# Output projection of a decoder layer with tokens on the partitions, and the first FFN tiles in token halves

## The reference, cut to what matters

```python
o  = m @ w_out                       # m: the merged mixers, (512, 1024); w_out: (1024, 1024)
x1 = x + o * rsqrt(mean(o * o, -1) + eps) * norm_post_mix
h2 = x1 * rsqrt(mean(x1 * x1, -1) + eps) * norm_pre_ffn
f  = (silu(h2 @ w_gate) * (h2 @ w_up)) @ w_down      # hidden width 2816
y  = x1 + f * rsqrt(mean(f * f, -1) + eps) * norm_post_ffn
```

## Time and profile before

| what | value |
|---|---|
| timed executions, median of 3 | 1194.46 us |
| the profiled execution's own time | 1198.94 us |
| its span in the trace | 1197.0 us |
| PE busy (matmul) | 1104.0 us, 92% |
| DVE, ACT, POOL busy | 575.0, 385.5, 504.9 us |
| share of PE in the chain that ended last | 61% |

### The profile page before, as it was taken

One profiled execution on the slowest core, in us unless ns is written; L12 is line 12 of the kernel. 1 busy time (PEld: TensorE's weight loads), 2 busy tenths in 40 slices (PEclk: granted clock), 3 DMA queues, 4 the chain that ended last, 5 costly groups with the idle time before them and its releaser, 6 DMA issues.

```text
span 1197.0 us, 19098 instructions
## 1 busy us (share of the span) xinstructions
PE 1104.0 (92%) x7610; PEld 851.6 (71%) x7610; DVE 575.0 (48%) x919; ACT 385.5 (32%) x679; POOL 504.9 (42%) x431
## 2 busy tenths in 40 slices
PE   5999898989996799999999899869999999999996
PEld 3775677777775566666767677747788788888885
DVE  4886745363564343445443676565344344331113
ACT  4122221212100433444443443244433433432222
POOL 1443322122233645665686445353444444434442
PEclk9998999999998999999999999979999999999998
DMA  7333112101143544122112436212233233222331
GB/s 216 92 88 71 51 31 51 23 19 29 55 124 106 167 127 125 53 54 62 28 36 62 149 115 202 71 53 67 85 94 101 83 97 97 81 67 89 96 91 75
DMA packets 172045, 101.30 MB, mean 85 GB/s; under 512 B 20997, under 2 KB 162575, under 8 KB 171976
## 3 DMA queue, kind: packets, MB, share of 16 engines
q1 hardware_dynamic: 168336, 95.44, 27.8%
q10 hardware_dynamic: 3608, 4.88, 1.7%
q0 software_dynamic: 32, 0.00, 0.0%
HBM read 92.67 MB, written 7.63 MB: 84 GB/s over the span
## 4 chain that ended last, share of the span: by engine, by line
PE 61%; issue 13%; DVE 11%; POOL 10%; ACT 2%; DMA 1%; POOLq 0%; DVEq 0%; ACTq 0%; SPq 0%
PE ps L1436 15%; PE ps L1438 13%; PE ps L1437 13%; POOL WLO L531 7%; PE ps L1569 5%; PE ps L1482 3%; PE ps L1721 2%; PE ps L1768 2%; DVE XF L1174 1%; DVE MT L1322 1%; POOL EB L592 1%; PE ps L1560 1%; DVE OT L1356 1%; POOL WLO L566 1%; DMA PRAW<-in_par 1%
## 5 line engine op out<-in xcount | busy, mean ns | idle before, releaser
L531 POOL TENSOR_TENSOR WLO<-WRAW,WHI 128x1024 fp32r<-128x1024 f32 (+3 forms) x156 | 331.2, 2123 | 390.2 <-ACT WHI L868 214.9
L1436 PE MATMUL ps<-HHI,WHI 128*128 128x512 f32 x792 | 331.5, 419 | 32.8 <-DVE HLO L1366 10.7
L1438 PE MATMUL ps<-HHI,WLO 128*128 128x512 f32 x792 | 311.8, 394 | 0.0
L1437 PE MATMUL ps<-HLO,WHI 128*128 128x512 f32 x792 | 311.7, 394 | 0.0
L1436 PEld LDWEIGHTS ps<-HHI,WHI 128*128 128x128 f32 x792 | 150.3, 190 | 99.3 <-issue 41.3
L1438 PEld LDWEIGHTS ps<-HHI,WLO 128*128 128x128 f32 x792 | 150.3, 190 | 33.0
L1437 PEld LDWEIGHTS ps<-HLO,WHI 128*128 128x128 f32 x792 | 150.6, 190 | 28.3 <-issue 2.3
L535 POOL CAST WHI<-WRAW 128x256 fp32r<-128x256 f32 (+1 forms) x83 | 48.9, 590 | 210.6 <-PE ps L1438 210.6
L868 ACT ACTIVATE WHI<-WRAW 128x1024 fp32r<-128x1024 f32 (+2 forms) x74 | 69.7, 941 | 137.2 <-PE ps L1438 137.1
L640 ACT ACTIVATE WHI<-WRAW 128x1024 fp32r<-128x1024 f32 (+1 forms) x57 | 50.0, 877 | 177.2 <-PE ps L1438 164.5
L1380 DVE TENSOR_TENSOR FT<-FT 128x512 f32<-128x512 f32 x22 | 38.5, 1750 | 110.3 <-ACT FT L874 110.3
(11 more groups left out here) (285 smaller groups left out, 1689.7 us busy)
## 6 DMA issues: line engine op xcount, KB each, us to landing
WRAW<-in_w_in SPq DMA_DIRECT2D x47, 512.0 KB, 4.1
WRAW<-in_w_gate SPq DMA_DIRECT2D x22, 512.0 KB, 3.8
WRAW<-in_w_up SPq DMA_DIRECT2D x22, 512.0 KB, 3.9
WRAW<-in_w_down SPq DMA_DIRECT2D x16, 384.0 KB, 3.4
spilled<-SQ SPq DMA_DIRECT2D x21, 256.0 KB, 2.3
WRAW<-in_w_down SPq DMA_DIRECT2D x16, 320.0 KB, 3.1
...
```

The source lines that it names most:

```text
L531: return pool.tensor_tensor(WLO[:, n % NSPL, 0:chunks, :], WRAW[:, n % NRAW, 0:chunks, :], WHI[:, n % NSPL, 0:chunks, :].bitcast(F32), ALU ...
L1436: pe.matmul(dst, WHI[:, s, k, :], hi, start=start, stop=False)
L1437: pe.matmul(dst, WHI[:, s, k, :], lo, start=False, stop=False)
L1438: return pe.matmul(dst, WLO[:, s, k, :], hi, start=False, stop=stop)
```

## The change

- The output product is turned round. The merged activations (MHI, MLO, a block of 128 tokens) become the stationary operand and 512 columns of `w_out` the moving one, so that a result bank holds 128 tokens on partitions by 512 channels (`out_product`, `out_bank`). A job is now two input chunks by 512 output columns. Jobs OUT0 to OUT0+3 make the left half of the channels for all four token blocks t at once, in four banks; jobs OUT0+4 to OUT0+7 make the right half, one token block after the other, in four further banks.
- Four more weight slots (XWHI, XWLO; `HOME`, `FREE`) hold jobs OUT0+2 to OUT0+5 and later FF0 and FF0+1, so that the weights of four jobs lie ready at once.
- The norm of a token block is a number per partition: ACT squares each bank with a sum along the free axis (`out_stats`), roots and reciprocals are of one column. `x_out(t)` on DVE scales from PSUM by that number and by the gain, read in by a DMA to all partitions (GPM). POOL adds XTOK in token layout; the result X1TOK is kept for the end of the kernel. The 32 transposes of x, the copies to OT and X1 and the sums in SSUM are gone, and so are the 32 transposes and 8 copies before the down stage.
- PE transposes X1TOK (`x1_transposes`), for token blocks 0 and 1 in the middle of the last block's output product, for blocks 2 and 3 after two half tiles of the FFN.
- HHI and HLO are made straight from PSUM in blocks of 256 tokens (`h2_high`, `h2_low`), and tiles FF0 and FF0+1 run as two halves of 256 tokens each.
- The second norm's factors (XRINV, one column per token block) are written on the diagonals of a matrix (DIAG, in SSUM) and spread over all partitions by one matmul with ones.
- The loads of x and of the gain are issued after the load of job OUT0+7, not after that of OUT0+3.

```diff
+HOME = {OUT0 + 2: NSPL, OUT0 + 3: NSPL + 1, OUT0 + 4: NSPL + 2, OUT0 + 5: NSPL + 3, FF0: NSPL, FF0 + 1: NSPL + 1}
+FREE = {OUT0 + 2: OUT0, OUT0 + 3: OUT0, OUT0 + 4: OUT0, OUT0 + 5: OUT0, OUT0 + 6: OUT0 + 1, OUT0 + 7: OUT0 + 2,
+        FF0: OUT0 + 3, FF0 + 1: OUT0 + 4, FF0 + 2: FF0, FF0 + 3: FF0}
...
-    OT = at("OT", 40, [P, KC, T])
-    X1 = at("X1", 116, [P, KC, T])
+    XWHI = at("XWHI", 40, [P, 4, 8, P], F32R)
+    XWLO = at("XWLO", 56, [P, 4, 8, P], F32R)
+    GPM = at("GPM", 16, [P, D])
+    OX = at("OX", 100, [P, 2, D])
+    X1TOK = at("X1TOK", 116, [P, 4, D])
...
-    X1TOK = Region(Z - 16 * KB).take("X1TOK", [P, 4, D])
...
+    def out_bank(t, dh):
+        return psum[(2, 3, 4, 5, 0, 1, 6, 7)[4 * dh + t]]
+    def x1_block(h, k):
+        return psum[(2, 3, 0, 1, 2, 3, 4, 6)[4 * h + k // 2]][:, 256 * (k % 2):256 * (k % 2) + 256]
...
-            return [(every, full, chunked(w_out, P * i))]
+            return [(every, full, chunked(w_out, T * (i // 4), T)[:, 2 * (i % 4):2 * (i % 4) + 2, :])]
...
-                if n == OUT0 + 3:
-                    sp.wait_ge(dense_done, OUT0)
-                    sp.dma_start(XTOK[:, :, :], x.rearrange("(t p) d -> p t d", p=P)).then_inc(xtok_in, 16)
+            sp.wait_ge(dense_done, OUT0)
+            sp.dma_start(XTOK[:, :, :], x.rearrange("(t p) d -> p t d", p=P)).then_inc(xtok_in, 16)
+            sp.dma_start(GPM[:, :], bass.AP(par1.tensor, par1.offset + P * PAR["g_post_mix"], [[0, P], [1, D]])).then_inc(gpm_in, 16)
...
                 if u == 2:
-                    for k in range(KC):
-                        pool.wait_ge(o_scaled, k + 1)
-                        pool.tensor_tensor(X1[:, k, :], X1[:, k, :], OT[:, k, :], ALU.add).then_inc(x1_ok, 1)
+                    pool.wait_ge(xtok_in, 32)
+                    for n in range(8):
+                        t, cols = n // 2, slice(T * (n % 2), T * (n % 2) + T)
+                        pool.wait_ge(ox_ok, n + 1)
+                        pool.tensor_tensor(X1TOK[:, t, cols], OX[:, t % 2, cols], XTOK[:, t, cols], ALU.add).then_inc(x1_ok, 1)
...
-                    act.wait_ge(dense_done, n - NSPL + 1)
+                    act.wait_ge(dense_done, slot_free(n))
...
-            for d in range(KC):
-                if n < FF0:
-                    hi_part(n)
-                    n += 1
-                act.wait_ge(dense_evac, group_of(OUT0 + d) + 1)
-                if d >= 2:
-                    act.wait_ge(out_sum, d - 1)
-                act.activation(SQ[:, d % 2, :], OT[:, d, :], ACT.Square).then_inc(out_sq, 1)
...
-            act.wait_ge(norm_ss, 2)
-            act.activation(SQ[:, 0, :], R[4][:, :], ACT.Sqrt, scale=1.0 / D, bias=EPSC[:, 0:1]).then_inc(norm_std, 1)
-            first_hi(1)
-            act.wait_ge(norm_rinv, 1)
-            for k in range(KC):
-                act.wait_ge(x1_ok, k + 1)
-                act.activation(HHI[:, k, :], X1[:, k, :], ACT.Identity, scale=par("g_pre_ffn", k)).then_inc(h2hi_ok, 1)
-                if k >= 2:
-                    act.wait_ge(x1_ss, k - 1)
-                act.activation(SQ[:, k % 2, :], X1[:, k, :], ACT.Square).then_inc(x1_sq, 1)
-            act.wait_ge(norm_ss, 3)
-            act.activation(SQ[:, 0, :], R[4][:, :], ACT.Sqrt, scale=1.0 / D, bias=EPSC[:, 0:1]).then_inc(norm_std, 1)
...
+            assert n == OUT0 + 2
+            for n in range(OUT0 + 2, FF0):
+                hi_part(n)
+            act.wait_ge(dense_done, OUT0 + 4)
+            for t in range(4):
+                if t >= 2:
+                    act.wait_ge(o_sq, t - 1)
+                act.activation(SQ[:, t % 2, :], out_bank(t, 0)[:, :], ACT.Square, accum_out=OSS[:, t:t + 1]).then_inc(o_sq, 1)
+            hi_part(FF0)
+            hi_part(FF0 + 1)
+            def out_stats(t):
+                if t < 3:
+                    act.wait_ge(out_t, t + 1)
+                else:
+                    act.wait_ge(dense_done, FF0)
+                act.wait_ge(o_sq, 3 + t)
+                act.activation(SQ[:, t % 2, :], out_bank(t, 1)[:, :], ACT.Square, accum_out=OSS[:, 4 + t:5 + t]).then_inc(o_sq, 1)
+                act.wait_ge(o_sq, 5 + t)
+                act.wait_ge(o_bias, 1)
+                act.activation(OSTD[:, t:t + 1], OSS[:, 4 + t:5 + t], ACT.Sqrt, scale=1.0 / D,
+                               bias=OBIAS[:, t:t + 1]).then_inc(o_std, 1)
+            def x1_stats(t):
+                act.wait_ge(x1_ok, 2 * t + 2)
+                act.activation(XTOK[:, t, :], X1TOK[:, t, :], ACT.Square,
+                               accum_out=XSS[:, t:t + 1]).then_inc(x1_sq, 1)
+            def h2_high(h):
+                act.wait_ge(x1T, 2 * h + 2)
+                for k in range(KC):
+                    act.activation(HHI[:, k, 256 * h:256 * h + 256], x1_block(h, k), ACT.Identity,
+                                   scale=par("g_pre_ffn", k)).then_inc(h2hi_ok, 1)
+            out_stats(0)
+            out_stats(1)
+            x1_stats(0)
+            out_stats(2)
+            x1_stats(1)
+            h2_high(0)
+            out_stats(3)
+            x1_stats(2)
+            h2_high(1)
+            x1_stats(3)
+            act.wait_ge(x1_sq, 4)
+            act.activation(XRINV, XSS, ACT.Sqrt, scale=1.0 / D, bias=EPSC[:, 0:1]).then_inc(x1_std, 1)
+            hi_part(FF0 + 2)
+            hi_part(FF0 + 3)
...
+            ffn_act(0, 0)
+            hi_loop(FF0 + 4, 0, 8)
+            hi_loop(FF0 + 5, 0, 8)
+            ffn_act(1, 0)
...
-            act.wait_ge(dense_done, DN0)
-            for n in range(0, 8, 2):
-                act.wait_ge(x1T, KC + n + 1)
-                act.activation(X1TOK[:, n // 2, 0:512], R[2 + n % 4][:, :], ACT.Copy).then_inc(tok_act, 1)
...
-            for d in range(KC):
-                if d == 5:
-                    for k in range(KC):
-                        dve.wait_ge(x1T, k + 1)
-                        dve.tensor_copy(X1[:, k, :], R[k % 4][:, :]).then_inc(x1T_ok, 1)
-                dve.wait_ge(dense_done, n + 1)
-                dve.tensor_copy(OT[:, d, :], DB[group_of(n) % 2][:, :]).then_inc(dense_evac, 1)
-                dve.wait_ge(dense_evac, group_of(n) + 1)
-                n += 1
-                if d == KC - 1:
-                    continue
-                dve.wait_ge(out_sq, d + 1)
-                if d == 0:
-                    dve.tensor_copy(SSUM[:, :], SQ[:, 0, :]).then_inc(out_sum, 1)
-                else:
-                    dve.wait_ge(out_sum, d)
-                    dve.tensor_tensor(SSUM[:, :], SSUM[:, :], SQ[:, d % 2, :], ALU.add).then_inc(out_sum, 1)
-            assert n == FF0
-            dve.wait_ge(norm_std, 2)
-            dve.reciprocal(RINV[:, :], SQ[:, 0, :]).then_inc(norm_rinv, 1)
+            dve.wait_ge(o_sq, 4)
+            dve.tensor_scalar(OBIAS, OSS[:, 0:4], 1.0 / D, EPS, ALU.mult, ALU.add).then_inc(o_bias, 1)
+            dve.wait_ge(gpm_in, 16)
+            def x_out(t):
+                dve.wait_ge(o_std, t + 1)
+                link(dve.reciprocal(ORINV[:, t:t + 1], OSTD[:, t:t + 1]))
+                for dh in range(2):
+                    if t >= 2:
+                        dve.wait_ge(x1_ok, 2 * (t - 2) + dh + 1)
+                    cols = slice(T * dh, T * dh + T)
+                    dve.scalar_tensor_tensor(out=OX[:, t % 2, cols], in0=out_bank(t, dh)[:, :], scalar=ORINV[:, t:t + 1],
+                                             in1=GPM[:, cols], op0=ALU.mult, op1=ALU.mult).then_inc(ox_ok, 1)
+            def h2_low(h):
+                for k in range(KC):
+                    dve.wait_ge(h2hi_ok, 8 * h + 2 * (k // 2) + 2)
+                    cols = slice(256 * h, 256 * h + 256)
+                    dve.scalar_tensor_tensor(out=HLO[:, k, cols], in0=x1_block(h, k), scalar=par("g_pre_ffn", k),
+                                             in1=HHI[:, k, cols].bitcast(F32), op0=ALU.mult, op1=ALU.subtract).then_inc(h2lo_ok, 1)
+            x_out(0)
+            x_out(1)
+            x_out(2)
+            h2_low(0)
+            x_out(3)
+            h2_low(1)
+            dve.wait_ge(x1_std, 1)
+            link(dve.reciprocal(XRINV, XRINV))
+            for t in range(4):
+                dve.tensor_scalar(DIAG[:, t, :], ident, XRINV[:, t:t + 1], None, ALU.mult).then_inc(diag_ok, 1)
+            dve.wait_ge(norm_ss, 2)
+            dve.tensor_copy(RINV[:, :], R[5][:, :]).then_inc(norm_rinv, 1)
...
-            for k in range(KC):
-                if k + 2 < KC:
-                    scale_o(k + 2)
-                dve.wait_ge(h2hi_ok, k + 1)
-                dve.scalar_tensor_tensor(out=HLO[:, k, :], in0=X1[:, k, :], scalar=par("g_pre_ffn", k),
-                                         in1=HHI[:, k, :].bitcast(F32), op0=ALU.mult, op1=ALU.subtract).then_inc(h2lo_ok, 1)
-            dve.wait_ge(norm_std, 3)
-            dve.reciprocal(RINV[:, :], SQ[:, 0, :]).then_inc(norm_rinv, 1)
-            dve.wait_ge(norm_rinv, 2)
...
-            dve.wait_ge(dense_done, DN0)
-            for n in range(1, 8, 2):
```

(84 more changed lines are left out.)

65 lines of the change are left out of this document (26 added, 39 removed).

## The result

The kernel after the change takes 1161.57 us, the median of four executions (1157.94 to 1165.52); the kernel before, beside it, took 1195.10 (1194.15 to 1195.77, four executions). The ratio is 0.9711 with a 95% interval of 0.9685 to 0.9736, so it is faster, by 33.5 us. By the ratio it is just outside: on the median from which the prediction was made that is 0.9711 x 1194.46 = 1159.9, 1 us under the low end of 1161. The change gained more than was foreseen, and the question is where. The profiled execution after took 1164.61 us with a span of 1162.7, where before had 1198.94 and 1197.0: 34.3 us between the two profiles.

A forecast was written before the change was run, and what follows sets the result against it. PE's own work was taken to bound the FFN and down stages, with waits at the sub-layers' join. Gains of 24.95 (7.2 in the output stage) and 4.55 make 29.5 us: 1194.46 - 29.5 = 1165.0, range 1161 to 1172.

The forecast's parts named there:

- The FFN loop and the down stage: FFN loop's written-out first pass gains nothing; dropping transposes and waits before the down stage gains 4.55 us.
- The output stage: Output product keeps its matmul spacing with operands turned round and ends at 778.0 instead of 785.2, 7.2 us less.
- Rival (d): Turned-round output product does not keep 0.226 us a matmul; at double spacing it costs 43.4 us, 1208.4; chance 0.02.
- The chain to x1_ok 4: Norm, scaling and POOL's adds for token block 1 end at 771.7, half a microsecond before PE needs them at 772.2.
- The loads: XTOK lands in 7.8 us, the gain in 2 (upper bound 10.9); FF0+1 is there by 758.4, before ACT asks at 758.9.
- rival (b): The gain's DMA or FF0's weights hold ACT; PE waits 3 to 5 us at 772, clock falls: 1171.5; chance 0.08.
- The half tiles: First two FFN tiles as 256-column matmuls run 0.12 us apart, 48 of them in 5.8 us.
- Rival (a): Weight loads limit the half tiles at 0.19 us a matmul, 6.7 us more less 0.4 hidden: 1171.3; chance 0.09.
- ACT and DVE in pairs: FFN input's high and low parts take 0.44 us per 256-column block, ending 778.6; PE, free at 778.0, waits 0.7.
- The second wait: PE waits about 1.6 us at 786.4, at the transposes of token blocks 2 and 3 and their input parts.
- rival (c): Short waits of 0.7 at 778 and about 1.6 at 786.4 let the clock fall once, 2 to 3 us: 1167.5; chance 0.10.
- The tail: Before the down stage 4.70 us of transposes and waits fall away, 0.15 comes back: gain 4.55 us.

The follow-up runs named there:

- e1: The kernel before with one two-column Sigmoid on ACT ahead of the FFN loop: 1189.7 us, ratio 0.9935 to before.
- e2: The kernel before with only ACT's first pass of the FFN loop written out: 1189.72 us, ratio 0.9934 to before.
- e3: The kernel after with a two-column Sqrt on ACT between the written-out first pass and the FFN loop: 1172.02 us, ratio 0.9771 to before.
- e5: The kernel after with the loads of x and the gain issued four jobs sooner, behind OUT0+3: 1161.22 us, ratio 0.9705 to before.
- e4: The kernel after with the first two FFN tiles whole, after the transposes of all token blocks: 1164.15 us, ratio 0.9732 to before.
- e7: The kernel after with the output product's right half made for all four token blocks at once: 1173.69 us, ratio 0.9802 to before.

## Why the prediction was right and where it failed

**The failed step.** In "The FFN loop and the down stage" the text says of the written-out first pass "The order of the loop is the same", and prices it at nothing with the reason that the gate values were not late. The order is the same; what ACT holds on entering the loop is not, and e1, e2 and e3 put the price at 6.6, 7.3 and 8.0 us where the sum had 0. The step looked at who waits at the loop's entry, and not at what each pass did. Behind it stands the first reading of the prediction, that in this stretch "only PE's own work counts", and the prediction's own numbers speak against that: 42 tiles at 5.43 us are 228.1, and the stretch took 235.3. The earlier trace rows has 3.95 us in which PE was idle there, and with the loads' two groups at ten each and the nine waits for the low part that gap had an owner. A load of 1283 ns was even used, once, for the norm's root. With this term at the 6.8 measured the sum would have been 36.3, and the stretch gave 37.0.

The Trainium skill (ScalarE activation tables: per-element evaluation and per-set limits, section Table sets in the compiler and the runtime) says that the compiler places table loads per block. The trace agrees: where ACT could come to the top of the loop's body from a Sqrt or from a Sigmoid there were two loads in every pass, where only from a Sigmoid there were none. Which table each load brings, and why one stands at the copy, no trace shows.

**The output stage.** Forecast 778.0 - 732.6 = 45.4 us, measured 45.5. 192 matmuls with the operands turned round keep their spacing. Rival (d), a slower spacing, did not happen.

**The chain to x1_ok 4.** The prediction gave it half a microsecond of margin. POOL's second pair of adds in the kernel after:

```profile
770.42 2.54 POOL L646 TENSOR_TENSOR X1TOK<-OX,XTOK 128x512 f32<-128x512 f32 x2 [1.49 <-DVE OX L1400]
```

It ends at 772.96, and PE asks at 774.95, so the margin is 2.0 us. The adds take 1.29 each on average, not the 1.71 of the earlier trace rows.

**The loads.** XTOK took 10.0 us from issue to landing (forecast 7.8) and the gain 11.2: not the 2 that I took but a little over its upper bound of 10.9. They overlapped each other and the weights, and ACT made the high parts of both first FFN tiles at 759.76 without a wait. The price of the gain was wrong by a factor of over five (8.8 us in e5, so over four there), and adding transfers one behind the other was wrong too; rival (b) still did not occur, and e5 shows how much room there is.

**The half tiles.** Forecast 0.12 a matmul, measured 0.122. Rival (a) is out. The Trainium skill's rule that a weight load overlaps a matmul only into another row group (TensorE: Matmul & The Clock Gate, section The mechanism) would have put these matmuls further apart, and here too the trace does not agree. The same section also lets PE pull a load ahead of running matmuls when it goes to the background weight buffer, which the prediction left out, and with that the trace agrees: the loads are recorded with 0.19 us each and the matmuls start 0.122 apart.

**ACT and DVE in pairs.** Eight blocks of 256 columns, ACT and then DVE in the kernel after:

```profile
776.89 3.03 ACT L904 ACTIVATE HHI<-ps,PARC 128x256 fp32r<-128x256 f32 x8 [1.05 <-PE ps L1525]
```

```profile
777.76 3.23 DVE L1408 SCALAR_TENSOR_TENSOR HLO<-ps,PARC,HHI 128x256 fp32r<-128x256 f32 x8 [1.33 <-ACT HHI L904]
```

0.38 and 0.40 a block, not 0.44. DVE's eight end at 780.99, and the first FFN matmul starts at 781.05, 0.47 behind the last of the product where the stream has 0.23: of the wait of 0.7 that was forecast there 0.2 was left. The second wait, forecast at about 1.6, was 1.45. From the product's end to the third FFN tile are 16.4 us where 17.3 were forecast; less 0.1 more in the product this is the 0.85 by which the join did better.

**The clock.** It stood at 1.00 through waits of up to 1.45 us, so rival (c) fell away. It did fall behind 3.47 in e4 and 6.47 in e7, as it did before behind 3.03 and 10.16.

**The tail.** 4.7 us gone and 0.2 back in the down stage, 4.5 net; forecast 4.55.

**The base.** The sum was taken from 1194.46, the median of three. Medians of 11 to 15 executions of the same kernel were 1196.0 to 1199.13, so the base was low by 1.5 to 4.7 us. If the 37.0 us of the stretch are the whole gain, 1161.57 belongs to a base of 1198.6, 4.1 above the one used. The gain was 7.5 us short and the base 4.1 low, the two errors partly cancel, and the point came within 3.4 us for a reason that is luck and not the prediction's merit. Whether the base was low by chance in three executions, or those ran under other conditions than the later sets, is not shown.
